# Sixteen 64 x 64 triangular inversions, one factor turned on TensorE instead of multiplied out

## The chip, the cores and the metric

The kernel runs on one core of one Trainium2 chip. The metric is the device time of one execution in microseconds (us), lower is better. It is one long program: two transformer layers, then a third "hybrid" block with a chunked linear recurrence. The change touches one stage of that block.

## The reference, cut to what matters

The hybrid block splits 512 positions into 8 chunks of 64. For every head and chunk a unit lower triangular 64 x 64 system has to be solved before the chunks can be chained:

```python
def _chunk_gated_delta_rule(q, k, v, beta, g):
    ...
    A = jnp.where(strict, jnp.einsum('bhnld,bhnmd->bhnlm', k, k) * decay * beta[..., :, None], 0.0)
    rhs = jnp.concatenate([v * beta[..., None], k * (beta * jnp.exp(gc))[..., None]], axis=-1)
    sol = lax.linalg.triangular_solve(A + jnp.eye(L, dtype=A.dtype), rhs,
                                      left_side=True, lower=True, unit_diagonal=True)
```

The other half of the heads follow the rule of `rwkv7_time_mix`, a step by step scan in the reference, which the kernel brings into the same chunked form with an A of its own.

## The kernel before, in words

The stage is the function `chunk_operators` (names with `ops_` in the trace). It works through 6 **pairs** of heads, i = 0 to 5 (`PAIRS`): pairs 0 to 2 are the RWKV kind, pairs 3 to 5 the gated delta kind (`delta(i)`). A pair has 2 heads h, 8 chunks as 4 tiles t of 2 halves c, so 16 matrices of 64 x 64. A tile of 128 partitions and 512 columns holds all of them: half c of the partitions holds the chunks of parity c, and unit u = 4h + t is a block of 64 columns.

The inverse T of I + A is built in five **levels** (lv 0 to 4), with U, its transpose, kept beside it. Each level takes the part M of A that joins blocks twice as large (POOL, `mask`), and then:

- TensorE (PE), `invert_x`, L2589: XT = M'U, 16 products of 64 x 64;
- ScalarE (ACT), `xt_out`, L2712: XT copied from PSUM to SBUF;
- PE, `invert_p`, L2601: PT = T'XT, and L2606: P = (XT)'T, 16 products each, P not on the last level;
- VectorE (DVE), `update`, L2885: U = U - PT, and L2889: T = T - P.

Between these stand, in an order written out by hand for every engine, the work that finishes the pair before (`finish_wu`, `finish_qm`, `finish_yn` on PE; `wu_out`, `yn_out` on ACT; `qm_out` on DVE) and the work that sets up the next (`setup_*` on PE; `tokens`, `a_out`, `ar_out`, `akr_out`, `init`, `delta_rows` on DVE; `decay_masks`, `diagonal`, `chunk_ends` on POOL). Each engine runs its own list from top to bottom, and semaphores tie the lists together. "Next pair is delta" holds for i = 2, 3, 4: there DVE's `tokens(i + 1)` builds the decays, ACT takes their exponentials, POOL masks them, and POOL's mask for level 3 stands behind those two.

A matrix product written once in the code shows in the trace as two instructions (x32 for 16 products); a transposition shows as one. A product on contraction half c that writes output half c uses two of the array's four quarters over a whole group; the order `DIAG` lets 16 products go round all four quarters, as `finish_qm` (L2542, L2549) does.

Of the kernel before, what the change touches and what calls it, by code (L numbers as in the profile page):

```python
# [20 lines left out]
ALU = mybir.AluOpType  # L21
# [2302 lines left out]
def chunk_operators(k, pi, bi, kr, ki, mt, n0, pc, el, rows, cols):  # L2324
# [5 lines left out]
    with Stage(k, "ops") as st:  # L2330
        slot = [k.H[:, j, :].rearrange("p (u m) -> p u m", m=CHUNK) for j in range(8)]
        A, T, U = slot[0:2], slot[2:4], slot[4:6]
# [12 lines left out]
        XT_B, P_B, PT_B = 0, 1, 2  # L2345
# [3 lines left out]
                 "t_init", "u_init", "chain", "xt_ps", "xt_out", "p_ps", "t_out", "pt_ps", "u_out", "wu_ps", "wu_out", "qm_ps",  # L2349
# [36 lines left out]
        def compact(bk):  # L2386
            return ps[:, bk, :].rearrange("p (u m) -> p u m", m=CHUNK)

# [12 lines left out]
        with k.nc.Block() as block:  # L2401
            @block.tensor
            def _(pe):
# [120 lines left out]
                def finish_wu(i):  # L2524
                    pe.wait_ge(s["u_out"], LV * (i + 1))
                    if not delta(i):
                        pe.wait_ge(s["x1_out"], i + 1)
                    if i:
                        pe.wait_ge(s["yn_out"], 2 * i)
                    for t in range(TT):  # L2530
                        for h in range(2):
                            u = TT * h + t
                            for c in range(2):
                                mm = pe.matmul(units(F0 + h)[half(c), t, :], U[i % 2][half(c), u, :], kx[half(c), i % 2, u, :], start=True, stop=True)
                    mm.then_inc(s["wu_ps"], 1)
# [42 lines left out]
                def invert_x(i, lv):  # L2578
                    n = LV * i + lv
                    pe.wait_ge(s["masked"], n + 1)  # L2580
                    if lv:
                        pe.wait_ge(s["u_out"], n)
                    else:
                        pe.wait_ge(s["u_init"], i + 1)
                        if i:
                            pe.wait_ge(s["xt_out"], n)
                    for u in range(U8):
                        for c in range(2):
                            mm = pe.matmul(compact(XT_B)[half(c), u, :], M[half(c), u, :], U[i % 2][half(c), u, :], start=True, stop=True)  # L2589
                    mm.then_inc(s["xt_ps"], 1)  # L2590

                def invert_p(i, lv):
                    n = LV * i + lv
                    pe.wait_ge(s["xt_out"], n + 1)
                    if lv:
                        pe.wait_ge(s["t_out"], 4 * i + lv)
                    else:
                        pe.wait_ge(s["t_init"], i + 1)
# [13 lines left out]
                for i in range(PAIRS):  # L2612
                    nxt = i + 1 < PAIRS
                    invert_x(i, 0)
                    if i:
                        finish_wu(i - 1)
                    else:
                        setup_akr(0)
# [7 lines left out]
                    invert_x(i, 1)  # L2626
                    if i:
                        finish_yn(i - 1)
# [3 lines left out]
                    invert_x(i, 2)  # L2632
                    if nxt:
                        setup_a(i + 1)
# [3 lines left out]
                    invert_x(i, 3)  # L2638
                    if nxt and not delta(i + 1):
                        setup_akr(i + 1)  # L2640
                    invert_p(i, 3)
                    invert_x(i, 4)
                    if nxt and not delta(i + 1):
                        setup_x1(i + 1)
# [8 lines left out]
            def _(act):  # L2653
# [52 lines left out]
                def xt_out(i, lv):  # L2706
                    n = LV * i + lv
                    act.wait_ge(s["xt_ps"], n + 1)
                    if n:
                        act.wait_ge(s["pt_ps"], n)  # L2710
                        act.wait_ge(s["p_ps"], 4 * i + lv)
                    act.activation(XT, compact(XT_B), ACT.Copy).then_inc(s["xt_out"], 1)  # L2712
# [78 lines left out]
            def _(dve):  # L2791
# [73 lines left out]
                def init(i):  # L2865
                    dve.wait_ge(s["a_out"], 2 * i + 2)
                    if i >= 2:
                        dve.wait_ge(s["wu_ps"], i - 1)
                        dve.wait_ge(s["pt_ps"], LV * (i - 1))
                    dve.tensor_tensor(T[i % 2], A[i % 2], over(level(0)), ALU.mult).then_inc(s["chain"], 1)  # L2870
                    dve.wait_ge(s["ar_out"], 2 * i + 2)
                    if delta(i):
                        dve.tensor_tensor(U[i % 2], ar[:, i % 2, :, 0, :], over(k.c("up0")[:, 0:CHUNK]), ALU.mult).then_inc(s["chain"], 1)
                    chained = i + max(i - MIX_T, 0)
                    dve.wait_ge(s["chain"], chained + 1)
                    dve.tensor_tensor(T[i % 2], over(k.c("ident2")), T[i % 2], ALU.subtract).then_inc(s["t_init"], 1)
                    if delta(i):
                        dve.wait_ge(s["chain"], chained + 2)
                    dve.tensor_tensor(U[i % 2], over(k.c("ident2")), U[i % 2] if delta(i) else ar[:, i % 2, :, 0, :], ALU.subtract).then_inc(s["u_init"], 1)

                def update(i, lv):
                    n = LV * i + lv
                    dve.wait_ge(s["pt_ps"], n + 1)
                    dve.wait_ge(s["u_out"], n) if lv else dve.wait_ge(s["u_init"], i + 1)
                    dve.tensor_tensor(U[i % 2], U[i % 2], compact(PT_B), ALU.subtract).then_inc(s["u_out"], 1)  # L2885
                    if lv < LV - 1:
                        dve.wait_ge(s["p_ps"], 4 * i + lv + 1)
                        dve.wait_ge(s["t_out"], 4 * i + lv) if lv else dve.wait_ge(s["t_init"], i + 1)
                        dve.tensor_tensor(T[i % 2], T[i % 2], compact(P_B), ALU.subtract).then_inc(s["t_out"], 1)  # L2889
# [22 lines left out]
                for i in range(PAIRS):  # L2912
                    nxt = i + 1 < PAIRS
                    if i == 0:
                        akr_out(0)
                    update(i, 0)
                    if i:
# [3 lines left out]
                    update(i, 1)  # L2921
                    if nxt and delta(i + 1):
# [3 lines left out]
                    update(i, 2)  # L2926
                    if nxt:
# [3 lines left out]
                    update(i, 3)  # L2931
                    if nxt:
# [799 lines left out]
```

## Time and profile before

| | |
|---|---|
| median of 3 runs | 2220.4 us (2219.17 to 2224.8) |
| the profiled execution | 2219.96 us, span 2218.2 us |
| the stage, first product to last | 1561.27 to 1733.67 us, 172.4 us |
| PE busy over the span | 97% |
| DVE / ACT / POOL busy over the span | 58% / 41% / 5% |
| mean granted TensorE clock | 0.995 |

The span is the time from the first to the last instruction; a row of the trace gives a start counted from the start of the span.

### The profile page before, as it was taken

Reading aid. Unit: us, or ns where it says so; the run is one execution under the profiler, and the core shown is the slowest. Engines: PE = TensorE matmul, PEld = TensorE weight load, DVE = VectorE, ACT = ScalarE, POOL = GpSimd, SP = SyncE. Lnnn points to the kernel's source line nnn. Section 1 sums busy time; section 2 is a strip of 40 time slices with the busy share of each in tenths; the row PEclk is TensorE's granted clock in tenths of the full one; section 3 lists DMA queues with packets and bytes.
Section 4 is the critical chain, followed back from the end, with each engine's and each line's share of the span. In section 5 each row is a group of like instructions: output and inputs, shape, how many; then the busy total and the mean of one; then the engine's idle time right before and its main releaser. Section 6 shows DMA issues by size and latency. Waiting matters only on the chain. (4 is left out here: it accounts for less than half of the span.)

```text
span 2218.2 us, 35739 instructions
## 1 busy us (share of the span) xinstructions
PE 2156.5 (97%) x14078; PEld 1724.8 (78%) x14078; DVE 1289.6 (58%) x1733; ACT 907.7 (41%) x1421; POOL 119.6 (5%) x96
## 2 busy tenths in 40 slices
PE   8999999999999999999999998999898899999999
PEld 6787788888877777778888876777787566888887
DVE  6564576663377877476665347686465566333333
ACT  4444532222365666642222244654222545323321
POOL 0000011110000000001110000000333000000000
PEclk9999999999999999999999999999999999999999
DMA  6331233333324321323333331322000112333331
GB/s 255 105 117 55 76 114 96 100 97 95 95 77 133 92 65 47 105 76 105 96 100 97 95 95 50 101 85 76 3 4 4 47 39 67 104 95 104 95 95 66
DMA packets 54087, 189.77 MB, mean 86 GB/s; under 512 B 5968, under 2 KB 6224, under 8 KB 53840
## 3 DMA queue, kind: packets, MB, share of 16 engines
q1 hardware_dynamic: 53680, 187.49, 27.5%
q8 instruction: 88, 1.44, 0.3%
q10 hardware_dynamic: 288, 0.59, 0.1%
q14 instruction: 31, 0.25, 0.0%
HBM read 184.91 MB, written 3.15 MB: 85 GB/s over the span
## 5 line engine op out<-in xcount | busy, mean ns | idle before, releaser
L299 PE MATMUL l_banks<-l_r_hi,l_w_hi 128*128 128x512 f32 x1440 | 574.7, 399 | 3.6 <-DVE l_r_lo L1796 2.3
L301 PE MATMUL l_banks<-l_r_hi,l_w_lo 128*128 128x512 f32 x1440 | 561.3, 390 | 0.0
L300 PE MATMUL l_banks<-l_r_lo,l_w_hi 128*128 128x512 f32 x1440 | 561.0, 390 | 0.0
L284 DVE TENSOR_TENSOR l_w_lo<-ring,l_w_hi 128x1024 fp32r<-128x1024 f32 x216 | 299.0, 1386 | 96.8 <-ACT l_w_hi L278 93.0
L278 ACT ACTIVATE l_w_hi<-ring 128x1024 fp32r<-128x1024 f32 x216 | 227.1, 1056 | 291.3 <-PE l_banks L301 286.5
L299 PEld LDWEIGHTS l_banks<-l_r_hi,l_w_hi 128*128 128x128 f32 x1440 | 270.6, 188 | 72.9 <-issue 8.4
L300 PEld LDWEIGHTS l_banks<-l_r_lo,l_w_hi 128*128 128x128 f32 x1440 | 270.8, 188 | 57.9 <-issue 4.3
L301 PEld LDWEIGHTS l_banks<-l_r_hi,l_w_lo 128*128 128x128 f32 x1440 | 270.5, 188 | 57.0
L299 PE MATMUL ff_banks<-ff_r_hi,ff_w_hi 128*128 128x512 f32 x512 | 200.0, 391 | 0.0
L300 PE MATMUL ff_banks<-ff_r_lo,ff_w_hi 128*128 128x512 f32 x512 | 199.2, 389 | 0.0
L301 PE MATMUL ff_banks<-ff_r_hi,ff_w_lo 128*128 128x512 f32 x512 | 199.2, 389 | 0.0
L735 POOL TENSOR_TENSOR tail_mid<-H 128x512 f32 x44 | 60.0, 1363 | 1143.9 <-ACT H L728 772.0
L284 DVE TENSOR_TENSOR ff_w_lo<-ring,ff_w_hi 128x1024 fp32r<-128x1024 f32 x64 | 78.3, 1225 | 61.7 <-ACT ff_w_hi L278 58.4
L299 PEld LDWEIGHTS ff_banks<-ff_r_hi,ff_w_hi 128*128 128x128 f32 x512 | 96.1, 188 | 20.4 <-issue 0.5
L300 PEld LDWEIGHTS ff_banks<-ff_r_lo,ff_w_hi 128*128 128x128 f32 x512 | 96.1, 188 | 20.3 <-issue 0.5
L301 PEld LDWEIGHTS ff_banks<-ff_r_hi,ff_w_lo 128*128 128x128 f32 x512 | 96.1, 188 | 20.2
L292 DVE TENSOR_TENSOR l_r_lo<-tail_mid,l_r_hi 128x512 fp32r<-128x512 f32 x44 | 30.5, 692 | 130.3 <-ACT l_r_hi L288 130.3
L299 PE MATMUL in_acc<-in_r_hi,in_w_hi 128*128 128x512 f32 x216 | 90.9, 421 | 0.0
L288 ACT ACTIVATE l_r_hi<-tail_mid 128x512 fp32r (+1 forms) x44 | 27.7, 630 | 153.1 <-PE l_banks L301 153.1
L301 PE MATMUL in_acc<-in_r_hi,in_w_lo 128*128 128x512 f32 x216 | 85.0, 393 | 0.0
L300 PE MATMUL in_acc<-in_r_lo,in_w_hi 128*128 128x512 f32 x216 | 84.7, 392 | 0.0
L292 DVE TENSOR_TENSOR ff_r_lo<-mid,ff_r_hi 128x512 fp32r<-128x512 f32 x32 | 22.2, 692 | 101.6 <-ACT ff_r_hi L288 101.6
(513 smaller groups left out, 3255.2 us busy)
## 6 DMA issues: line engine op xcount, KB each, us to landing
ring<-weights SPq DMA_DIRECT2D x315, 512.0 KB, 3.6
na_bias<-window_bias SPq DMA_DIRECT2D x16, 512.0 KB, 5.4
da_rel<-t_rel SPq DMA_DIRECT2D x8, 448.0 KB, 4.2
outT<-X SPq DMA_DIRECT2D x12, 256.0 KB, 2.1
X<-xT SPq DMA_DIRECT2D x8, 256.0 KB, 5.7
const<-consts SPq DMA_DIRECT2D x1, 1312.0 KB, 11.5
l_pt<-pT SPq DMA_DIRECT2D x2, 512.0 KB, 4.3
X<-outT SPq DMA_DIRECT2D x4, 256.0 KB, 3.3
```

Of the source, the lines that this page charges most:

```text
L278: act.activation(self.w_hi[:, c % self.slots, :], k.ring[:, g % RING, :], ACT.Copy).then_inc(self.w_rounded, 1)
L284: dve.tensor_tensor(self.w_lo[:, c % self.slots, :], k.ring[:, g % RING, :], self.w_hi[:, c % self.slots, :].bitcast(F32), ALU.subtract).t ...
L288: act.activation(self.hi(slot), src, ACT.Copy).then_inc(self.rhs_rounded, 1)
L292: dve.tensor_tensor(self.lo(slot), src, self.hi(slot).bitcast(F32), ALU.subtract).then_inc(self.rhs_split, 1)
L299: pe.matmul(psum, hi, self.hi(rhs_slot), start=start, stop=False)
L300: pe.matmul(psum, hi, self.lo(rhs_slot), start=False, stop=False)
L301: return pe.matmul(psum, lo, self.hi(rhs_slot), start=False, stop=stop)
L735: pool.tensor_tensor(mid[:, f + j, :], gelu[:, j, :], value[:, j, :], ALU.mult).then_inc(mid_done, 1)
```

## The change

U's columns are ordered tile, head, column, so that the two heads of one tile stand side by side. XT is written to the partition half of its head instead of its chunk, so that `invert_x` and `invert_p` both go over four quarters in the order `DIAG`. T is no longer updated: on every level `turn_u` transposes U, four transpositions of 128 x 128 behind `invert_x`, and DVE copies the result to T (`turned_out`). The product P, the update of T and the making of the first T in `init` are gone. `invert_x` of level 0 now also waits for the last update of the pair before.

```diff
-                    for u in range(U8):
-                        for c in range(2):
-                            mm = pe.matmul(compact(XT_B)[half(c), u, :], M[half(c), u, :], U[i % 2][half(c), u, :], start=True, stop=True)
+                def turn_u(i, lv):
+                    n = LV * i + lv
+                    if lv:
+                        pe.wait_ge(s["u_out"], n)
+                    else:
+                        pe.wait_ge(s["u_init"], i + 1)
+                    if n:
+                        pe.wait_ge(s["t_out"], n)
+                    for t in range(TT):
+                        mm = pe.transpose(units(TURN_B)[:, t, :], U[i % 2][:, :, t, :].rearrange("p h m -> p (h m)"), k.c("ident"))
+                    mm.then_inc(s["t_ps"], 1)
+                def invert_x(i, lv):
+                    n = LV * i + lv
+                    pe.wait_ge(s["masked"], n + 1)
+                    if n:
+                        pe.wait_ge(s["u_out"], n)
+                    if lv == 0:
+                        pe.wait_ge(s["u_init"], i + 1)
+                    for t in range(TT):
+                        for pair in DIAG:
+                            for c, h in pair:
+                                mm = pe.matmul(xt_ps(c, t)[half(h)], M[half(c), TT * h + t, :], U[i % 2][half(c), h, t, :], start=True, stop=True)
                     mm.then_inc(s["xt_ps"], 1)
...
                 def invert_p(i, lv):
                     n = LV * i + lv
                     pe.wait_ge(s["xt_out"], n + 1)
-                    for u in range(U8):
-                        for c in range(2):
-                            mm = pe.matmul(compact(PT_B)[half(c), u, :], T[i % 2][half(c), u, :], XT[half(c), u, :], start=True, stop=True)
+                    pe.wait_ge(s["t_out"], n + 1)
+                    for t in range(TT):
+                        for pair in DIAG:
+                            for c, h in pair:
+                                mm = pe.matmul(pt_ps(h, t)[half(c)], T[i % 2][half(h), 2 * t + c, :], XT[half(h), TT * c + t, :], start=True, stop=True)
                     mm.then_inc(s["pt_ps"], 1)
-                    if lv < LV - 1:
-                        for u in range(U8):
-                            for c in range(2):
-                                mm = pe.matmul(compact(P_B)[half(c), u, :], XT[half(c), u, :], T[i % 2][half(c), u, :], start=True, stop=True)
-                        mm.then_inc(s["p_ps"], 1)
...
+                def turned_out(i, lv):
+                    n = LV * i + lv
+                    dve.wait_ge(s["t_ps"], n + 1)
+                    if n:
+                        dve.wait_ge(s["pt_ps"], n)
+                    dve.tensor_copy(T[i % 2], compact(TURN_B)).then_inc(s["t_out"], 1)
...
                 for i in range(PAIRS):
                     nxt = i + 1 < PAIRS
+                    turned_out(i, 0)
                     if i == 0:
                         akr_out(0)
                     update(i, 0)
+                    turned_out(i, 1)
                     if i:
                         qm_out(i - 1)
                     if nxt and delta(i + 1):
                         delta_rows(i + 1)
                     update(i, 1)
+                    turned_out(i, 2)
                     if nxt and delta(i + 1):
                         tokens(i + 1)
                     if nxt:
                         a_out(i + 1)
                     update(i, 2)
+                    turned_out(i, 3)
                     if nxt:
                         ar_out(i + 1)
                         if not delta(i + 1):
                             akr_out(i + 1)
                     update(i, 3)
+                    turned_out(i, 4)
                     if nxt:
                         init(i + 1)
                     update(i, 4)
```

What stands in a row on an engine moves as follows. On PE, levels 2 and 3 of pair 0, whose next is RWKV; L2414 and in the changed kernel L2430 are `setup_a`, `setup_ar` and `setup_akr`. Before:

```order
L2589 MATMUL ops_ps<-H 64x64 x16
L2414 MATMUL ops_ps<-bi,kr 64x64 x16
L2601 MATMUL ops_ps<-H 64x64 x16
L2606 MATMUL ops_ps<-H 64x64 x16
L2414 MATMUL ops_ps<-kr,bi 64x128 x16
L2589 MATMUL ops_ps<-H 64x64 x16
L2414 MATMUL ops_ps<-kr,ki 64x128 x16
L2601 MATMUL ops_ps<-H 64x64 x16
L2606 MATMUL ops_ps<-H 64x64 x16
```

In the changed kernel, with L2617 for XT, L2604 for the transpositions and L2627 for PT:

```order
L2617 MATMUL ops_ps<-H 64x64 x16
L2604 MATMUL ops_ps<-const,H 128x128 x4
L2430 MATMUL ops_ps<-bi,kr 64x64 x16
L2627 MATMUL ops_ps<-H 64x64 x16
L2430 MATMUL ops_ps<-kr,bi 64x128 x16
L2617 MATMUL ops_ps<-H 64x64 x16
L2604 MATMUL ops_ps<-const,H 128x128 x4
L2430 MATMUL ops_ps<-kr,ki 64x128 x16
L2627 MATMUL ops_ps<-H 64x64 x16
```

The transpositions stand between XT and the set-up product of each level; the second product of `invert_p` is gone.

On DVE, levels 1 and 2 of pair 2, whose next is delta; L2813 to L2825 are `tokens`, L2837 is `a_out`. Before:

```order
L2885 TENSOR_TENSOR H<-H,ops_ps 128x512
L2889 TENSOR_TENSOR H<-H,ops_ps 128x512
L2813 TENSOR_TENSOR ops_akr<-ops_ps,cols 128x512
L2817 TENSOR_SCALAR ops_akr<-ops_akr 128x512
L2819 TENSOR_SCALAR ops_akr<-ops_akr 128x512
L2823 TENSOR_TENSOR ops_kx<-ops_ps,cols 128x8x64 x2
L2825 TENSOR_TENSOR ops_v_tok<-ops_ps,cols 128x2x4x64
L2837 TENSOR_TENSOR H<-ops_ps,ops_akr 128x256 x2
L2885 TENSOR_TENSOR H<-H,ops_ps 128x512
L2889 TENSOR_TENSOR H<-H,ops_ps 128x512
```

In the changed kernel, with L2912 for the update of U, L2906 for the copy of T, L2838 to L2850 for `tokens` and L2862 for `a_out`:

```order
L2912 TENSOR_TENSOR H<-H,ops_ps 128x2x4x64
L2906 COPY H<-ops_ps 128x512
L2838 TENSOR_TENSOR ops_akr<-ops_ps,cols 128x512
L2842 TENSOR_SCALAR ops_akr<-ops_akr 128x512
L2844 TENSOR_SCALAR ops_akr<-ops_akr 128x512
L2848 TENSOR_TENSOR ops_kx<-ops_ps,cols 128x8x64 x2
L2850 TENSOR_TENSOR ops_v_tok<-ops_ps,cols 128x2x4x64
L2862 TENSOR_TENSOR H<-ops_ps,ops_akr 128x256 x2
L2912 TENSOR_TENSOR H<-H,ops_ps 128x2x4x64
L2906 COPY H<-ops_ps 128x512
```

The row ahead of `tokens` was the update of T for level 1 and is now the copy of T for level 2, which needs the transpositions of level 2.

## Rows read from the trace of the kernel before

**Rows 1.** Windows: busy time of each engine over the stage (windows view)

```profile
1561.27:1733.67 172.40, 148.97 (x4524) 134.74 (x4524) 91.94 (x144) 44.17 (x77) 59.39 (x48) 0.98 0.02 4
```

The columns are the stretch, its length, busy time with instructions of PE, PE weight loads, DVE, ACT and POOL, the granted clock, DMA share and GB/s.

**Rows 2.** Timeline of pair 5, level 3: start, duration, engine, line [idle before]

```profile
1719.06 1.15 PE L2589 MATMUL ops_ps<-H 64*64 64x64 f32 x32
...
1720.24 0.60 ACT L2712 ACTIVATE H<-ops_ps 128x512 f32<-128x512 f32 x1 [3.27 <-PE ops_ps L2589]
...
1720.89 1.15 PE L2601 MATMUL ops_ps<-H 64*64 64x64 f32 x32 [0.69 <-ACT H L2712]
...
1722.09 0.69 DVE L2885 TENSOR_TENSOR H<-H,ops_ps 128x512 f32<-128x512 f32 x1 [2.24 <-PE ops_ps L2601]
...
1722.92 1.15 PE L2589 MATMUL ops_ps<-H 64*64 64x64 f32 x32
```

**Rows 3.** Timeline and groups: four-quarter product, copy from PSUM, transpositions

```profile
1729.84 0.69 PE L2542 MATMUL ops_ps<-ops_ar,ops_wu 64*64 64x64 f32 x32 [1.18 <-ACT ops_wu L2693]
...
L1850 DVE COPY tail_m<-l_banks 128x512 f32<-128x512 f32 x8 | 5.3, 685 | 1.4 <-ACT H L1753 1.4
...
1614.49 1.13 PE L2601 MATMUL ops_ps<-H 64*64 64x64 f32 x32
...
1615.55 0.66 PE L2406 MATMUL ops_ps<-const,bi 128*128 128x128 f32 x4
...
1616.57 1.15 PE L2589 MATMUL ops_ps<-H 64*64 64x64 f32 x32
```

**Rows 4.** Timeline of pair 4, level 2 (next pair is delta)

```profile
1689.88 0.69 DVE L2813 TENSOR_TENSOR ops_akr<-ops_ps,cols 128x512 f32<-128x512 f32 x1 [0.57 <-PE ops_ps L2442]
...
1690.79 1.15 PE L2589 MATMUL ops_ps<-H 64*64 64x64 f32 x32
...
1692.76 1.27 POOL L2752 TENSOR_TENSOR ops_akr<-ops_akr,const 128x512 f32<-128x512 f32 x1 [5.62 <-ACT ops_akr L2662]
...
1695.22 1.28 POOL L2770 TENSOR_TENSOR H<-H,const 128x512 f32<-128x512 f32 x1
...
1696.55 0.62 PE L2589 MATMUL ops_ps<-H 64*64 64x64 f32 x14 [0.38 <-POOL H L2770]
```

**Rows 5.** Timeline of pair 1, levels 2 and 3 (next pair is RWKV)

```profile
1603.69 1.09 PE L2589 MATMUL ops_ps<-H 64*64 64x64 f32 x30
...
1608.33 1.10 PE L2589 MATMUL ops_ps<-H 64*64 64x64 f32 x32
1608.57 1.29 DVE L2842 TENSOR_TENSOR ops_ar<-ops_ps,const 128x512 f32<-128x512 f32 x2 [0.22 <-PE ops_ps L2414]
1609.41 1.10 PE L2414 MATMUL ops_ps<-kr,ki 64*64 64x128 f32 x32
...
1610.57 1.29 DVE L2842 TENSOR_TENSOR ops_akr<-ops_ps,const 128x512 f32<-128x512 f32 x2 [0.71 <-PE ops_ps L2414]
...
1612.60 1.15 PE L2589 MATMUL ops_ps<-H 64*64 64x64 f32 x32 [0.24 <-DVE H L2885]
```

**Rows 6.** Timeline of levels 0 and 1: pair 1, and the start of pair 4's level 1

```profile
1590.78 1.15 PE L2589 MATMUL ops_ps<-H 64*64 64x64 f32 x32
1591.76 1.92 PE L2534 MATMUL ops_ps<-ops_kx,H 64*64 64x128 f32 x32
...
1596.31 1.10 PE L2589 MATMUL ops_ps<-H 64*64 64x64 f32 x32
1596.56 0.69 DVE L2902 TENSOR_TENSOR bi<-ops_ps,kr 128x512 f32<-128x512 f32 x1 [0.28 <-PE ops_ps L2549]
...
1684.63 1.09 PE L2589 MATMUL ops_ps<-H 64*64 64x64 f32 x30
```

**Rows 7.** Timeline at the end of pair 3, and a windows row

```profile
1671.12 1.15 PE L2589 MATMUL ops_ps<-H 64*64 64x64 f32 x32
...
1675.48 1.88 PE L2589 MATMUL ops_ps<-H 64*64 64x64 f32 x32 [1.38 <-issue]
...
1675.63:1679.05 3.42, 3.42 (x51) 3.42 (x51) 0.35 (x1) 0.60 (x1) 1.26 (x1) 0.50 0.00 0
```

More of the change, by code:

```diff
@@ L2331, in chunk_operators @@
         slot = [k.H[:, j, :].rearrange("p (u m) -> p u m", m=CHUNK) for j in range(8)]
-        A, T, U = slot[0:2], slot[2:4], slot[4:6]
+        A, T = slot[0:2], slot[2:4]
+        U = [k.H[:, j, :].rearrange("p (t h m) -> p h t m", h=2, m=CHUNK) for j in (4, 5)]
         XT, M = slot[6], slot[7]
@@ L2344, in chunk_operators @@
         ps = st.ps("ps", [P, 8, S])
-        XT_B, P_B, PT_B = 0, 1, 2
+        TURN_B = 2
         SETUP = (3, 4, 7)
@@ L2348, in chunk_operators @@
         names = ("turned", "tok_out", "keys_turned", "key_out", "a_ps", "a_out", "ar_ps", "ar_out", "akr_ps", "akr_out", "x1_ps", "x1_out", "masked",
-                 "t_init", "u_init", "chain", "xt_ps", "xt_out", "p_ps", "t_out", "pt_ps", "u_out", "wu_ps", "wu_out", "qm_ps",
+                 "u_init", "chain", "xt_ps", "xt_out", "t_ps", "t_out", "pt_ps", "u_out", "wu_ps", "wu_out", "qm_ps",
                  "q_out", "mt_out", "yn_ps", "yn_out", "row_ps", "dif_done", "clamped", "exped", "dmask", "scaled", "di_done",
@@ L2387, in compact, with xt_ps, pt_ps, all_xt @@
             return ps[:, bk, :].rearrange("p (u m) -> p u m", m=CHUNK)
+        def xt_ps(c, t):
+            return ps[:, c, t * CHUNK:(t + 1) * CHUNK]
+        def pt_ps(h, t):
+            return ps[:, h, HALF + t * CHUNK:HALF + (t + 1) * CHUNK]
+        def all_xt():
+            return ps[:, 0:2, 0:HALF]
+        def all_pt():
+            return ps[:, 0:2, HALF:S].rearrange("p h (t m) -> p h t m", m=CHUNK)
+        def heads(x):
+            return x.rearrange("p (h t) m -> p h t m", h=2)
         def half(h):
@@ L2533, in finish_wu @@
                             for c in range(2):
-                                mm = pe.matmul(units(F0 + h)[half(c), t, :], U[i % 2][half(c), u, :], kx[half(c), i % 2, u, :], start=True, stop=True)
+                                mm = pe.matmul(units(F0 + h)[half(c), t, :], U[i % 2][half(c), h, t, :], kx[half(c), i % 2, u, :], start=True, stop=True)
                     mm.then_inc(s["wu_ps"], 1)
@@ L2614, in _ @@
                     invert_x(i, 0)
+                    turn_u(i, 0)
                     if i:
@@ L2626, in _ @@
                     invert_x(i, 1)
+                    turn_u(i, 1)
                     if i:
@@ L2632, in _ @@
                     invert_x(i, 2)
+                    turn_u(i, 2)
                     if nxt:
@@ L2638, in _ @@
                     invert_x(i, 3)
+                    turn_u(i, 3)
                     if nxt and not delta(i + 1):
@@ L2642, in _ @@
                     invert_x(i, 4)
+                    turn_u(i, 4)
                     if nxt and not delta(i + 1):
@@ L2710, in xt_out @@
                         act.wait_ge(s["pt_ps"], n)
-                        act.wait_ge(s["p_ps"], 4 * i + lv)
-                    act.activation(XT, compact(XT_B), ACT.Copy).then_inc(s["xt_out"], 1)
+                    act.activation(XT.rearrange("p (c t) m -> p c (t m)", c=2), all_xt(), ACT.Copy).then_inc(s["xt_out"], 1)
                 act.preload_act_table_set(LN_EXP)
@@ L2865, in init @@
                 def init(i):
-                    dve.wait_ge(s["a_out"], 2 * i + 2)
+                    dve.wait_ge(s["ar_out"], 2 * i + 2)
                     if i >= 2:
                         dve.wait_ge(s["wu_ps"], i - 1)
-                        dve.wait_ge(s["pt_ps"], LV * (i - 1))
-                    dve.tensor_tensor(T[i % 2], A[i % 2], over(level(0)), ALU.mult).then_inc(s["chain"], 1)
-                    dve.wait_ge(s["ar_out"], 2 * i + 2)
+                        dve.wait_ge(s["t_ps"], LV * (i - 1))
+                    u0, eye = heads(ar[:, i % 2, :, 0, :]), heads(over(k.c("ident2")))
                     if delta(i):
[L2873 to L2879, printed above, removed]
+                        dve.tensor_tensor(U[i % 2], u0, heads(over(k.c("up0")[:, 0:CHUNK])), ALU.mult).then_inc(s["chain"], 1)
+                        dve.wait_ge(s["chain"], i - MIX_T + 1)
+                    dve.tensor_tensor(U[i % 2], eye, U[i % 2] if delta(i) else u0, ALU.subtract).then_inc(s["u_init"], 1)
+                def turned_out(i, lv):
[4 more added lines that the diff above has]
+                    dve.tensor_copy(T[i % 2], compact(TURN_B)).then_inc(s["t_out"], 1)
                 def update(i, lv):
```

14 lines of the change are left out of this document (1 added, 13 removed).

## The prediction, as put on record before the changed kernel ran

> **What bounds the kernel now.** The page says that PE is busy 97% of the span. That is an average over a program that is nearly all large products. The change lives in one stage, so I read that stage alone: the windows view gives 172.40 us, PE busy 148.97, DVE 91.94, ACT 44.17, POOL 59.39 [rows 1]. PE is busy 86% there, and no engine is full. A stage like that is bound by a chain that passes from engine to engine, so the next view is the timeline, and what I measure in it is the distance from one XT product to the next: the length of a level. There are 30.
>
> The purest level is one with nothing but the inversion in it, in pair 5 [rows 2]. XT starts at 1719.06 and lasts 1.15; ACT starts 0.03 behind its end and takes 0.60; PT starts 0.05 behind that and lasts 1.15; DVE starts 0.05 behind its end and takes 0.69; the next XT starts at 1722.92. Length 3.86. The second product P and the update of T (PE's next in line, and DVE's) lie beside this chain, so their removal by itself gives next to nothing here; it gives something only where PE has set-up work queued behind P.
>
> **The prices of the new pieces.** A group of 16 products over four quarters lasts 0.69 (L2542) [rows 3] against 1.15 over two [rows 2]; it lets the next group start 0.46 earlier as well, so it holds the engine about 0.5 instead of about 1.0. Four transpositions last 0.66. Eight of them, from 1615.55, let the next product start at 1616.57, so four hold PE about 0.58, and the first starts 0.07 later than a plain product would behind the 16 at 1614.49 (0.99 apart) [rows 3]. The copy of a bank from PSUM on DVE takes 0.685 (L1850) [rows 3]. The new DVE and ACT access patterns I take at the old times, 0.69 and 0.60: they move as many elements.
>
> These changes of shape on PE are where a rule speaks against the change. The Trainium skill (TensorEngine Tiling (Array Packing), Key Properties) says that changing the tiling mode drains TensorE, and 30 turns add 60 changes. By the rows above such a pair of changes costs about 0.07 + 0.2, which is inside the 0.65 that I charge; if a change were free, a turn would hold PE about 0.4, and T would be ready 0.1 to 0.2 earlier.
>
> **The new plain level.** Counted from XT's start: XT's last product starts at 0.48, the transpositions start at 0.63 and end at 1.29, DVE copies T from 1.33 to 2.02, PT starts at 2.08 and ends at 2.77, DVE updates U to 3.50, the next XT starts at 3.56. The XT copy on ACT would have let PT start at 0.69 + 0.03 + 0.60 + 0.05 = 1.37, so it is now T, not XT, that comes last, by 0.7. So the shorter products would give 0.9 per level and the turn takes 0.6 back: 3.56 against 3.86.
>
> **The wait that the change adds.** DVE runs its list in order, and the copy of T for level n + 1 stands directly behind the update of U for level n, ahead of all other DVE work of that level. It can't run before the transpositions of that level. So any DVE work of the level starts at XT + 1.95 at the earliest. Before, the row that stood there was the update of T for the level just past, and the other work could start before XT or a quarter of a microsecond behind it. Where that work heads a chain, the level grows. Kind by kind:
>
> 1. *Level 2 with a delta pair next, three levels (i = 2, 3, 4).* Before: `tokens` starts at 1689.88, that is 0.91 before XT at 1690.79. Behind it in a chain: two clamps, two exponentials on ACT (XT's copy waits behind these too), two masks on POOL from 1692.76, then POOL's mask for level 3 at 1695.22 for 1.28, and the next XT at 1696.55, released by it [rows 4]. Length 5.76, all of it set by that chain, 6.67 from `tokens` to XT. After: `tokens` at XT + 1.95, next XT at 1.95 + 6.67 = 8.6. **+2.86 each, +8.6.** This is the largest term.
> 2. *Level 3 with an RWKV pair next, two levels (i = 0, 1).* Before: `ar_out` starts 0.24 behind XT, the `akr` product at 1.08, `akr_out` at 2.24, next XT at 4.27 [rows 5]. After: `ar_out` at 1.95; the `akr` product waits for its first half, 2.65, and lasts 1.15; `akr_out` from 3.85 to 5.14 (two evacuations, 1.29); update of U to 5.76; next XT at 5.8. **+1.55 each, +3.1.**
> 3. *Level 1 with a pair to finish, five levels.* Before, pair 1: `qm_out` starts 0.25 behind XT and `finish_yn` follows at about 1.6 [rows 6]. After: the two evacuations run from 1.95 to 3.24 and `finish_yn` starts at 3.34, 1.7 later. Against that, PT and P, two groups over two quarters, held PE about 1.9 in a row before `setup_tokens`, and now PT alone holds it 0.5 and the change of shape 0.1, 1.3 less: +0.4 for i = 1. For i = 2, 3, 4 the `qm_out` work had been hidden under `setup_rows` and `finish_yn` ran directly behind XT; the length was 6.16 at i = 4 [rows 6, 4]. After, for i = 4: 3.34, plus 1.0 for `finish_yn` (two groups over four quarters), plus 0.6 for PT and the change, plus 2.05 for `setup_tokens` (eight transpositions at 1.02 [rows 3], and four row products that I take as long again) = 7.0, +0.9, and I take the same for i = 2 and 3. For i = 5, without set-up, PT starts at 4.3 and the level ends 1.49 behind it, as in the plain level: 5.8 against the plain chain and 1.0 of `finish_yn`, 4.9: +0.9. **Together +4.0.** Level 1 of pair 0 has nothing to finish and gains 1.1.
> 4. *Level 2 with RWKV next, two levels.* 4.64 before [rows 5], held by PE; `a_out` (two evacuations of half the columns) now fits between the copy of T and the end of PT: 3.56. **-1.1 each, -2.2.**
> 5. *Level 0, five levels (i = 1 to 5).* 5.53 before [rows 6]: XT, then `finish_wu` for 1.92, PT, P, `finish_qm`. After: `finish_wu` from 1.21 to 3.16, its two copies on ACT (0.60 each with a little overlap, 1.1, which P used to hide) to 4.3, `finish_qm` (two groups over four quarters) 1.0: 5.3. **-0.2 to -0.3 each, -1.3.** T's copy is hidden under `finish_wu`.
> 6. *Level 4.* `init` has one operation instead of three (RWKV) or two instead of four (delta). Before 3.97 (1612.60 [rows 5] to 1616.57 [rows 3]) and 4.36 [rows 7]; after 3.78, held by `setup_keys` on PE, and 3.86. **-0.2 for two, -0.5 for three, -0.2 for the last: -2.1.**
> 7. *Plain levels 2 and 3 of pair 5*: -0.3 each, **-0.6.** Level 3 with a delta pair next: `ar_out` (1.29) behind T's copy gives 3.9 against the plain 3.86, **0.**
> 8. *Before the first XT*: two operations fewer in `init` are 1.3, of which POOL's list, which starts its second half at the `akr` product, keeps 0.2: **-1.1.**
>
> Sum: 8.6 + 3.1 + 4.0 - 1.1 - 2.2 - 1.3 - 2.1 - 0.6 - 1.1 = **+7.3 us.** The work removed from PE, some 33 us (in each of six pairs 14 groups of about 1.0 become 10 of 0.5 and 5 turns of 0.65), mostly turns into waiting.
>
> **The clock.** At 1675.63 the granted clock fell to 0.50, the 1.2 GHz level, for 3.42 us [rows 7]; just before, PE had done one product group in 3 us, because of `init`. XT took 1.88 instead of 1.15, and `finish_wu` about 1.0 more: 1.7 us. The level-4 wait shrinks, so this fall may go; but each level of kind 1 now has about 3 us in which PE has nothing between the transpositions and `setup_a`. Three such falls cost between nothing (the POOL chain sets the end there) and 1.7 each; I take 0.8 each and give back 1.7: +0.7. The Trainium skill (TensorE: Matmul & The Clock Gate, Part 1) has an idle or cold engine at half rate, and this trace agrees, by the row above.
>
> The profiled execution took 2219.96 us, 0.4 under the median. 2220.0 + 7.3 + 0.7 = **2228.0 us**, 0.34% over the median. A measurement here can tell about 0.3%, which is 6.7 us, so this is slower by just more than can be told.
>
> **The rivals.**
> - *The gains and losses nearly cancel* (30%). It needs the level-1 terms or the clock to be overstated: if item 3 is 0 instead of +4.0 and no clock falls, 2220.0 + 3.3 - 1.7 = 2221.6. For it: item 3 is the sum of several short overlaps. Against it: item 1 alone is 8.6 and rests on one row order and one chain. Range 2215 to 2226.9.
> - *PE's list is what holds most levels, and 33 us less of it wins* (10%). It would be so if DVE's late start were covered: then items 1 to 3 are no loss, and 2220.0 - 1.1 - 2.2 - 1.3 - 2.1 - 0.6 - 1.1 is 2211.6, and up to 4 less if level 3 gains as level 2 does. For it: PE is 86% busy [rows 1]. Against it: in the pure level of 3.86 PE waits 0.69 for ACT ahead of L2601 [rows 2], and would have to wait for DVE without P. It decides if `tokens` starts less than 0.5 behind XT.
> - *The clock stays low over long stretches* (10%). PE now works 0.5 + 0.6 + 0.5 = 1.6 in a plain level of 3.56 and waits the rest; the fall at 1675.63 came behind such waits. Against it: it came once in 30 levels. At half clock XT, turn and PT are each about 0.4 longer: 1.3 per level. Over 12 levels more that is 2228 + 15 = 2243.
> - *The copy of T collides with POOL's mask*, which starts 0.04 behind XT and lasts 1.27, over the copy (5%). Held until the mask's end, T comes 0.5 later on 29 levels: 2242. Against it: DVE reads PSUM here, and the update of U at 1722.09 took its 0.69 like any other [rows 2].
>
> My forecast itself has 45%, and its own range is 2226 to 2234. With the rivals the range that holds the time 8 times in 10 is 2218 to 2240: the cancelling case is nearly all in, the two slow ones in part, the fast one out. Chances: faster by over 0.3% 0.10, within 0.3% 0.32, slower by over 0.3% 0.58; the forecast lies so near the bound that a part of its own range counts as within.
>
> **What the profile of the changed kernel would show.** PT released by DVE's copy of T and not by ACT, about 2.08 behind XT; plain levels of 3.5 to 3.6; `tokens` (L2838) at about XT + 1.95 and the level-2 lengths of pairs 2, 3, 4 at 8 to 9; L2867's second pair on level 3 of pairs 0 and 1 starting near XT + 3.9; the stage 7 to 8 longer with PE busy some 30 us less. I am wrong if level 2 with delta next is under 6.5 (then the order on DVE isn't what I read), if plain levels are over 4 (collision or clock), or if products over four quarters take much more than 0.69 when PT waits on DVE.

## The result: 31 us slower, and most of it is clock

The changed kernel takes 2251.16 us (median of 4 runs, 2250.37 to 2251.37) against 2219.86: ratio 1.0135, 95% interval 1.0122 to 1.0149. The forecast was 2228 with a range to 2240: right in sign, far too small. Its profiled execution has a span of 2249.6 us.

The windows view of the stage in the changed kernel, with the columns of [rows 1]:

```profile
1561.53:1764.40 202.87, 149.54 (x3876) 124.81 (x3876) 82.81 (x138) 44.46 (x77) 58.34 (x48) 0.77 0.01 3
```

The stage grew from 172.40 to 202.87 us, 30.5 of the 31.4 us by which the span grew. PE has 648 instructions fewer than in [rows 1] and is busy just as long, 149.5 against 149.0 us. The column that moved is the granted clock: 0.98 before, 0.77 now. A busy time that doesn't fall when a seventh of the instructions is taken away is the first sign that each piece takes longer. The trace has the granted clock at 0.50, the 1.2 GHz level, in 92 us of the stage, against 6.8 us before.

A level with nothing but the inversion in it, at that clock, from PE's and DVE's timelines of pair 5 (one piece for each engine):

```profile
1745.12 1.14 PE L2617 MATMUL ops_ps<-H 64*64 64x64 f32 x32 [0.89 <-DVE H L2912]
1746.18 1.11 PE L2604 MATMUL ops_ps<-const,H 128*128 128x128 f32 x4
1748.17 1.13 PE L2627 MATMUL ops_ps<-H 64*64 64x64 f32 x32 [0.88 <-DVE H L2906]
1750.20 1.14 PE L2617 MATMUL ops_ps<-H 64*64 64x64 f32 x32 [0.89 <-DVE H L2912]
...
1747.34 0.69 DVE L2906 COPY H<-ops_ps 128x512 f32<-128x512 f32 x1 [2.36 <-PE ops_ps L2604]
1749.37 0.69 DVE L2912 TENSOR_TENSOR H<-H,ops_ps 128x512 f32<-128x512 f32 x1 [1.34 <-PE ops_ps L2627]
```

```profile
1740.04:1745.12 5.08, 3.31 (x68) 2.66 (x69) 1.38 (x2) 0.60 (x1) 1.27 (x1) 0.50 0.01 3
```

XT, the four transpositions and PT take 1.14, 1.11 and 1.13, where at full clock they take 0.69, 0.66 and 0.69. DVE's two operations still take 0.69. The level is 5.08 long against 3.86 in [rows 2]. XT over four quarters at half clock, 1.14, is no faster than XT over two quarters was at full clock, 1.15. The chain is the one forecast: PT is released by DVE's copy of T (L2906), and XT's copy on ACT no longer matters.

The two largest terms of the queue part of the forecast hold. Pair 3, level 2 (next pair is delta), where [rows 4] had 5.76:

```profile
1671.44 0.69 PE L2617 MATMUL ops_ps<-H 64*64 64x64 f32 x32
1672.06 0.66 PE L2604 MATMUL ops_ps<-const,H 128*128 128x128 f32 x4
1672.76 0.69 DVE L2906 COPY H<-ops_ps 128x512 f32<-128x512 f32 x1 [2.54 <-PE ops_ps L2604]
1673.37 0.68 DVE L2838 TENSOR_TENSOR ops_akr<-ops_ps,cols 128x512 f32<-128x512 f32 x1
...
1675.72 0.77 PE L2430 MATMUL ops_ps<-pi,kr 64*64 64x64 f32 x32 [2.99 <-DVE ops_kx L2848]
...
1676.23 1.27 POOL L2777 TENSOR_TENSOR ops_akr<-ops_akr,const 128x512 f32<-128x512 f32 x1 [12.14 <-ACT ops_akr L2688]
1676.69 1.13 PE L2627 MATMUL ops_ps<-H 64*64 64x64 f32 x32 [0.20 <-ACT H L2737]
...
1678.70 1.26 POOL L2795 TENSOR_TENSOR H<-H,const 128x512 f32<-128x512 f32 x1
1680.02 0.79 PE L2617 MATMUL ops_ps<-H 64*64 64x64 f32 x17
```

`tokens` (L2838) starts 1.93 behind XT (forecast 1.95), the next XT at 8.58 (forecast 8.6). PE stands still for 2.99 us ahead of `setup_a`. The clock falls at 1676.2, inside this level, PT takes 1.13, and the level is not a tenth longer for it, since POOL's masks set its end.

Pair 1, level 3 (next pair is RWKV), where [rows 5] had 4.27:

```profile
1608.60 0.71 PE L2617 MATMUL ops_ps<-H 64*64 64x64 f32 x32
...
1609.93 0.69 DVE L2906 COPY H<-ops_ps 128x512 f32<-128x512 f32 x1 [1.48 <-PE ops_ps L2604]
1610.54 1.28 DVE L2867 TENSOR_TENSOR ops_ar<-ops_ps,const 128x512 f32<-128x512 f32 x2
...
1611.36 1.10 PE L2430 MATMUL ops_ps<-kr,ki 64*64 64x128 f32 x32 [1.47 <-DVE ops_ar L2867]
...
1612.53 1.29 DVE L2867 TENSOR_TENSOR ops_akr<-ops_ps,const 128x512 f32<-128x512 f32 x2 [0.71 <-PE ops_ps L2430]
...
1614.55 0.65 PE L2617 MATMUL ops_ps<-H 64*64 64x64 f32 x29 [1.62 <-DVE H L2912]
```

The `akr` product waits for the first half of `ar_out`, which waits behind the copy of T; 5.95 against a forecast of 5.8.

### The profile page after: what moved, and what is told of

It is laid out like the page before. It is cut to its first block and busy times, and to the rows that moved or that the text cites. A ratio compares the mean times of both kernels' runs of the same rounds, so it can differ in the third digit from the quotient of the medians.

```text
span 2249.6 us, 34468 instructions
## 1 busy us (share of the span) xinstructions
PE 2158.5 (96%) x13430; PEld 1716.0 (76%) x13430; DVE 1280.5 (57%) x1727; ACT 908.3 (40%) x1421; POOL 118.6 (5%) x96
## 5 line engine op out<-in xcount | busy, mean ns | idle before, releaser
L292 DVE TENSOR_TENSOR l_r_lo<-tail_mid,l_r_hi 128x512 fp32r<-128x512 f32 x44 | 30.5, 692 | 130.3 <-ACT l_r_hi L288 130.3
```

The source lines that it names most:

```text
L292: dve.tensor_tensor(self.lo(slot), src, self.hi(slot).bitcast(F32), ALU.subtract).then_inc(self.rhs_split, 1)
```

## The experiments

**Theory:** two causes that add. The copy of T in DVE's list lengthens some levels (15.7 us by items 1 to 3 of the forecast, about 7 once the gains elsewhere are taken off), and PE, which now does its work in short bursts with waits between, is granted the half clock about half of the time (about 24 us). **Rivals:** the new pieces themselves are dear (changes of shape on the array, the copy against POOL's mask); or only one of the two causes is real. Each kernel was timed in five rounds or more beside the kernel before, which ran at 2220.5 to 2221.4.

### Fill the waits of PE

```diff
+                def warm(n, bk, at):
+                    for _ in range(n):
+                        pe.matmul(ps[:, bk, at:at + P], k.c("ident"), k.c("levels")[:, 0:P], start=True, stop=True)
...
                     turn_u(i, 3)
+                    warm(4 if nxt and not delta(i + 1) else 2, F0, 0)
...
                     invert_p(i, 3)
+                    warm(5 if nxt and not delta(i + 1) else 3, TURN_B, 0)
```

and likewise ahead of `finish_yn` (behind a wait for T's copy), on level 2 with a delta pair or none next, and on level 4.

> The changed kernel with products added whose result nobody reads (128 columns each, two to nine in a row), put into waits of PE: after the transpositions and after PT. Nothing else differs, and PE has more work. Clock theory: of the 31 us that the change cost, some 7 are the longer levels and some 24 the granted clock, which was 0.77 over the stage; with the waits filled the clock is at 0.95 or more in the stage and the time 2226 to 2233 us, near the 2228 forecast, although PE does more. Rival, the new pieces themselves are dear (change of shape on the array, copy of T against POOL's mask): the time stays at 2251 or rises by the added work, to 2255 or more.

Measured: 2236.27 us, ratio 1.0069 (1.0056 to 1.0083). Adding work to PE made the changed kernel 15 us faster. The plain level of pair 5 in the filled kernel, where L2632 are the filling products:

```profile
1734.01 0.69 PE L2617 MATMUL ops_ps<-H 64*64 64x64 f32 x32
1734.64 0.66 PE L2604 MATMUL ops_ps<-const,H 128*128 128x128 f32 x4
...
1734.81 1.27 POOL L2810 TENSOR_TENSOR H<-H,const 128x512 f32<-128x512 f32 x1 [2.47 <-PE ops_ps L2617]
...
1735.13 0.61 PE L2632 MATMUL ops_ps<-const 128*128 128x128 f32 x4
1735.33 0.69 DVE L2921 COPY H<-ops_ps 128x512 f32<-128x512 f32 x1 [1.46 <-PE ops_ps L2604]
...
1736.17 0.69 PE L2627 MATMUL ops_ps<-H 64*64 64x64 f32 x32 [0.43 <-DVE H L2921]
...
1736.92 0.69 DVE L2927 TENSOR_TENSOR H<-H,ops_ps 128x512 f32<-128x512 f32 x1 [0.90 <-PE ops_ps L2627]
1737.76 0.69 PE L2617 MATMUL ops_ps<-H 64*64 64x64 f32 x32
```

3.75 in place of 5.08, with the same chain. The four-quarter groups take 0.69, and the copy of T takes its 0.69 beside POOL's mask (L2810), so neither the new pieces nor that meeting is dear. The stage:

```profile
1561.47:1748.38 186.91, 156.77 (x4118) 133.12 (x4118) 82.42 (x138) 44.24 (x77) 58.41 (x48) 0.95 0.01 3
```

The clock is at 0.95 as expected, the time 3 us above the range given: 20 us at half clock are left, three quarters of it on level 1 of pairs 3 and 4, which took 11.55 and 9.68 there. The mean clock over the whole kernel was 0.990 to 0.993 in all five executions, against 0.975 to 0.977 in those of the changed kernel.

A second filling put products where the first had left falls:

```diff
                     invert_p(i, 0)
+                    warm(3 if i else 0, TURN_B, 0)
...
                     turn_u(i, 1)
+                    warm(0 if i else 3, F0, 0)
```

> The changed kernel with filling products put where the first filling left the clock to fall (pair 0 level 1, behind PT on level 0) and one fewer ahead of finish_yn. If the forecast of the schedule (7 us over before) is right and the rest is clock: stage clock over 0.96 and 2226 to 2232 us. If the filled kernel stays at 2236, some 8 us of the change are neither in the forecast's levels nor in the clock.

Measured: 2238.36 us, ratio 1.0076 (1.0062 to 1.0090). A miss: not under 2232. Its stage clock was 0.93, under the 0.96 that its forecast needed, with 27 us at half clock, 16 of them on level 1 of pairs 2 and 4 (10.39 and 10.63; pair 3's was 7.88). So the second filling doesn't settle the last 8 us by its time; the lengths of the single levels do, all but one, below.

### Another order on DVE, alone and with the filling

```diff
                     update(i, 1)
-                    turned_out(i, 2)
                     if nxt and delta(i + 1):
                         tokens(i + 1)
+                    turned_out(i, 2)
                     if nxt:
                         a_out(i + 1)
```

and likewise `qm_out` and `delta_rows` ahead of the copy on level 1, `ar_out` on level 3, `init` on level 4.

> The changed kernel with DVE's list alone in another order: qm_out and delta_rows ahead of the copy of T on level 1, tokens ahead of it on level 2, ar_out on level 3, init on level 4. Queue theory: level 2 with a delta pair next falls from 8.6 to about 5.8, level 3 with RWKV next from 5.9 to about 4.4, level 1 by 1 to 2; the stage is some 20 us shorter as far as the schedule goes. Part of it the clock may take, since PE's list is unchanged and levels of 3.5 leave PE waiting half the time: 2212 to 2232 us. Rival, the order on DVE does not matter and only the clock does: 2245 to 2255 us.

Measured: 2220.69 us, ratio 0.9997 (0.9988 to 1.0006). The four moves give back the whole loss, though the stage's clock is still low:

```profile
1561.29:1736.99 175.70, 140.12 (x3876) 115.76 (x3876) 84.07 (x138) 44.53 (x77) 57.95 (x48) 0.84 0.01 3
```

Level 2 of pair 2 in this kernel, 5.75 long:

```profile
1624.46 0.69 DVE L2838 TENSOR_TENSOR ops_akr<-ops_ps,cols 128x512 f32<-128x512 f32 x1 [0.32 <-PE ops_ps L2458]
...
1625.37 0.69 PE L2617 MATMUL ops_ps<-H 64*64 64x64 f32 x32
...
1627.79 0.68 DVE L2906 COPY H<-ops_ps 128x512 f32<-128x512 f32 x1
...
1631.12 0.58 PE L2617 MATMUL ops_ps<-H 64*64 64x64 f32 x24 [0.75 <-POOL H L2795]
```

`tokens` starts 0.91 ahead of XT again. The gain, 30 us, is more than the 15.7 that items 1 to 3 had put down to the copy's place, for two reasons that this run shows together: the new order also shortens level 1 below what it was before the change (5.78 for 7.78 in pair 2), and 57 us are at half clock instead of 92.

> Both of the edits before together. If the two causes add up: clock 0.95 or more in the stage and 2204 to 2214 us, below the kernel before. If the order alone already keeps PE busy enough, the filling gives nothing or costs up to 5 us against it.

Measured: 2226.42 us, ratio 1.0022 (1.0013 to 1.0031): worse than the new order without filling, outside the range given. The fault is in the edit: on level 1 the filling waits for T's copy, which in this order stands behind `qm_out` and `delta_rows`, so `finish_yn` went behind it too. Level 1 of pair 1 took 7.95 at full clock instead of 5.39, and pairs 2 and 3, with 6.8 us at half clock each, took 10.78 and 10.62 instead of 5.8; level 2 with a delta pair next took 6.45 instead of 5.75. It says nothing on whether the causes add.

> The changed kernel with the copy of T moved from DVE's list to ACT's, behind the copy of XT; DVE's list is as before without the update of T. Queue theory: as with the new order on DVE, level 2 with a delta pair next is at 5.8, level 3 with RWKV next at 4.3 to 4.5, and the time 2212 to 2226 us, with a low clock. If what lengthened those levels was not the copy's place on DVE, they stay at 8.6 and 5.9 and the time at 2245 to 2255.

The edit puts `turned_out` into ACT's list behind `xt_out` and takes it out of DVE's. Measured: 2215.61 us, ratio 0.9979 (0.9968 to 0.9990), inside the range given. Level 2 with a delta pair next is 5.76 and level 3 with RWKV next 4.4 to 4.5: a second way to the same lengths, with DVE's order otherwise untouched. The stage's clock was 0.88 there. What lengthened those levels was the copy's place in DVE's list.

### Keep P, and take P's work away

The four quarters stay, the turn stays on level 0 only, and P and the update of T come back:

```diff
                     mm.then_inc(s["pt_ps"], 1)
+                    if lv < LV - 1:
+                        for t in range(TT):
+                            for c in range(2):
+                                for h in range(2):
+                                    mm = pe.matmul(compact(TURN_B)[half(h), 2 * t + c, :], XT[half(h), TT * c + t, :], T[i % 2][half(h), 2 * t + c, :], start=True, stop=True)
+                        mm.then_inc(s["p_ps"], 1)
...
-                    turn_u(i, 1)
...
                     dve.tensor_tensor(U[i % 2], U[i % 2], all_pt(), ALU.subtract).then_inc(s["u_out"], 1)
+                    if lv < LV - 1:
+                        dve.wait_ge(s["p_ps"], 4 * i + lv + 1)
+                        dve.wait_ge(s["t_out"], n + 1)
+                        dve.tensor_tensor(T[i % 2], T[i % 2], compact(TURN_B), ALU.subtract).then_inc(s["t_out"], 1)
```

> The four-quarter XT and PT are kept, but T is turned from U on level 0 only, and then updated from P as before the change (P over two quarters behind PT, into the bank of the turn; T = T - P on DVE behind the update of U). DVE's list is then nearly that of before. If the turn on every level and its copy were what cost, this is faster than the kernel before: plain levels of 2.9 us in place of 3.86, about 2198 to 2208 us, with the clock at 0.95 or more since P keeps PE at work while DVE updates U. If four-quarter products themselves starve the clock, the stage's clock is 0.8 or so and the time 2215 to 2230 us.

Measured: 2207.20 us, ratio 0.9938 (0.9925 to 0.9952), faster than both kernels. A plain level of pair 5:

```profile
1707.14 0.69 PE L2617 MATMUL ops_ps<-H 64*64 64x64 f32 x32
...
1707.89 0.60 ACT L2740 ACTIVATE H<-ops_ps 128x512 f32<-128x512 f32 x1 [2.80 <-PE ops_ps L2617]
...
1708.54 0.69 PE L2627 MATMUL ops_ps<-H 64*64 64x64 f32 x32 [0.71 <-ACT H L2740]
1709.06 1.10 PE L2633 MATMUL ops_ps<-H 64*64 64x64 f32 x32
...
1709.30 0.69 DVE L2915 TENSOR_TENSOR H<-H,ops_ps 128x512 f32<-128x512 f32 x1 [1.47 <-PE ops_ps L2627]
1710.14 0.65 PE L2617 MATMUL ops_ps<-H 64*64 64x64 f32 x29
```

3.00 us. PT is released by ACT again at XT + 1.40; P (L2633) lies under DVE's update of U and costs the chain nothing. The stage is 158.4 us long at clock 0.97. So the four-quarter products are worth 0.86 on a plain level, and the turn on every level took 0.74 of it back (3.74 at full clock).

> The kernel that keeps P (2207 us), with work left out: on levels 1 to 3 only 2 of the 16 products of P are made, so T is updated from stale values and the output isn't the reference's. P lies beside the chain (DVE updates U meanwhile), so by the schedule this gives 0 to 2 us: 2205 to 2207 if the clock stays. Clock theory: P is what kept PE at work in those 18 levels, so the granted clock falls more often and the time RISES though work is taken away: 2210 to 2225 us, stage clock under 0.93. This is the reverse of the filling.

Measured: 2208.92 us, ratio 0.9947 (0.9933 to 0.9960), against 2207.20 and 0.9938 (0.9925 to 0.9952) with the work in. It lies under the range that the clock theory gave, and the two intervals overlap.

```profile
1562.16:1723.50 161.34, 126.22 (x4044) 108.28 (x4044) 84.82 (x138) 44.23 (x77) 58.04 (x48) 0.87 0.01 3
```

The clock part came as expected: 0.87, with 43 us at half clock instead of 10, and over the whole kernel 0.986 to 0.988 in all five executions against 0.993 to 0.995. The rise in time did not come: 1.7 us is too little to tell. Some levels were shorter at full clock (3.16 for 3.98 on level 1 of pair 0), and that paid for most of the clock. What it shows: with 504 PE instructions taken away the clock falls, and no time is gained.

> The kernel before with the same left out: on levels 1 to 3 only 2 of the 16 products of P, so the output isn't the reference's. It shows what P's removal alone is worth to the old kernel. Schedule: 5 to 7 us less, where PE had set-up work queued behind P: 2213 to 2215 us if the clock stays. Clock theory: some more falls than the one of before, each about 1.5 us where PE is on the path, since XT and PT over two quarters still hold PE 2 of 3.9 us: 2214 to 2222 us.

Measured: 2214.12 us, ratio 0.9970 (0.9961 to 0.9979), stage clock 0.98 as before, 6.8 us at half clock as before: the schedule's share came and no more time at half clock. So taking P away was not enough to bring the clock down where XT and PT went over two quarters; in the kernel with four quarters it was.

> The changed kernel with the order of its products alone altered: XT and PT do all the products of one diagonal first and then those of the other, so that only two quarters are in use at a time. Same products, same turn, same queues; a group holds PE about 1.0 us instead of 0.5. By the schedule at full clock that is 0.9 us more in each of about 25 levels, over 2250 + 20. Clock theory: a group over four quarters at half clock took 1.13 us in the changed kernel, no less than one over two quarters at full clock before (1.15), so the longer groups cost little where the clock was low and keep it high: stage clock over 0.93, time 2245 to 2262 us. Rival (the low clock comes from something else than how much of the time PE works): clock stays near 0.77 and the time goes over 2270.

```diff
-                    for t in range(TT):
-                        for pair in DIAG:
+                    for pair in DIAG:
+                        for t in range(TT):
```

Measured: 2260.57 us (2250.96 to 2264.60), ratio 1.0176 (1.0160 to 1.0193). In the profiled execution, 2251 us like the changed kernel's, XT over two quarters took 0.97 at full clock, and the plain level 4.30 against 3.74, so the nominal price is 0.28 a group, 60 groups, 17 us and not the 0.9 a level that I had expected; 9 of them were paid in the median and none in the profiled execution. Two groups of pair 5, level 3, and the stage:

```profile
1746.06 0.97 PE L2617 MATMUL ops_ps<-H 64*64 64x64 f32 x32 [0.88 <-DVE H L2912]
...
1748.49 0.98 PE L2627 MATMUL ops_ps<-H 64*64 64x64 f32 x32 [0.88 <-DVE H L2906]
```

```profile
1561.76:1763.68 201.92, 151.98 (x3876) 129.87 (x3876) 82.88 (x138) 44.20 (x77) 58.37 (x48) 0.89 0.01 3
```

The clock rose from 0.77 to 0.89, short of the 0.93 expected, with 46 us at half clock for 92. But this is the fastest of the five executions. Over the whole kernel its mean clock is 0.985, the other four had 0.977 to 0.984, the slower the lower, and the changed kernel had 0.975 to 0.977. So the clock rose clearly in two of the five and little in the others (median 0.979). How long PE is at work between the waits is thus at most part of the cause; with waits of the same 0.88 us as in the changed kernel, pair 5 ran at full clock up to its last XT in this execution.

### POOL's order

```diff
-                    if nxt and delta(i + 1):
-                        decay_masks(i + 1)
                     mask(i, 3)
+                    if nxt and delta(i + 1):
+                        decay_masks(i + 1)
```

> The kernel that keeps P, with POOL's mask for level 3 ahead of the two decay masks of the next pair. In the trace of the kernel that keeps P, level 2 with a delta pair next is still 5.76, as before the change, set by POOL. Expected: these three levels at about 4.9, 2 to 3 us in all, 2203 to 2206 us. If ACT's exponentials ahead of the XT copy set them as well, nothing: 2207.

Measured: 2203.92 us, ratio 0.9926 (0.9913 to 0.9940): the fastest median, 17 us under the kernel before, though its interval overlaps that of the kernel that keeps P. Level 2 with a delta pair next went from 5.76 to 5.11, 5.11 and 4.90, 2.2 us in all; two stretches of 3.4 us at half clock, on pair 1 and on pair 5, were gone too, which is chance or consequence, I can't tell which.

> The kernel before with only POOL's mask for level 3 ahead of the next pair's two decay masks. It says how much of the gain of that edit has nothing to do with the change. Expected: level 2 with a delta pair next from 5.76 to 5.3 or less, 1 to 2.5 us in all, 2218 to 2220 us.

Measured: 2221.57 us, ratio 1.0005 (0.9995 to 1.0014): nothing, and above the range given. The three levels did go to 5.32 and 5.33, and 13 us of the stage were at half clock instead of 6.8, six of them on level 0 of pair 0, which took 7.39 for 5.46.

## Why the prediction was wrong, step by step

The lengths of the levels, at full clock where any of the changed kernel and its two filled forms had them so (XT to XT, us):

| kind of level | before | forecast | changed, full clock |
|---|---|---|---|
| plain (pair 5, levels 2 and 3) | 3.86 | 3.56 | 3.74 |
| level 2, delta next, three | 5.76 | 8.6 | 8.6 |
| level 3, RWKV next, two | 4.28 | 5.8 | 5.9 |
| level 2, RWKV next, two | 4.63 | 3.56 | 3.74 |
| level 1, pair 0 | 4.88 | 3.8 | 3.81 |
| level 1, pair 1 | 7.38 | +0.4 | 7.93 |
| level 1, pairs 2 and 3 | 7.78, 8.06 | +0.9 | 7.95, 7.88 |
| level 1, pair 4 | 6.16 | 7.0 | none at full clock; 9.68 at best |
| level 1, pair 5 | 4.90 | 5.8 | 5.86 |
| level 0, pairs 1 and 5 | 5.53, 5.50 | 5.3 | 5.34 |
| level 0, pairs 2 to 4 | 7.53, 7.53, 9.15 (3.4 of it at half clock) | 5.3 | 7.36, 7.43, 7.36 |
| level 4, RWKV / delta next | 3.97 / 4.37 | 3.78 / 3.86 | 3.80 / 4.04 |

- **The queue terms (items 1 to 8) held as a sum.** Over the 29 distances between the 30 XTs the kernel before adds up to 155.4 us, or 153.7 with its one level at half clock taken at the 7.53 of its like. The changed kernel adds up to 183.9, and the lowest lengths of the three runs to 165.8, 2.7 of which are what the one level never seen at full clock took over its forecast of 7.0. With the first XT 1.6 us earlier in the stage, the schedule alone costs 8 to 10.5 us. The forecast was 7.3. The largest item, 1, came to the tenth (2.8 to 2.9 each). That the sum is so near is in part luck: item 3 was some 1.6 too dear if pair 4 took its 7.0, and items 4 to 7 promised some 2 us more than came.
- **The latency from DVE to PE** was taken as 0.06. Where PT and XT wait for DVE alone, it is 0.15 (U's update ends at 1737.61, XT starts at 1737.76 in the filled kernel). The plain level was 0.18 short for that. [rows 2] had 0.14 there (1722.09 + 0.69 to 1722.92), though with P in PE's list.
- **Item 3 was a little too dear**: +0.9 for pairs 2 and 3 was -0.2 to +0.2.
- **Item 5 misread three levels.** It took 5.53 for all five; level 0 of pairs 2 to 4, with set-up of a next pair in it, was 7.5. The gain was about the same, 0.1 to 0.2.
- **The failed step is "The clock".** It read the one fall of [rows 7] as the price of long waits only, gave the changed kernel three falls, in the levels of kind 1, and +0.7 us. There were 92 us at half clock. The stage grew by 30.5, of which 8 to 10.5 are the schedule, so the clock cost 20 to 23 us more than before. Of the three levels that it named, two lost nothing by the clock, as its lower bound had it, because POOL sets their end, and pair 4's lost 0.6 (9.23 for 8.63). The time went elsewhere, by each level's length less its lowest at full clock, pair 4's level 1 taken at 7.0: some 11 us on levels 0 and 1, where PE also finishes one pair or sets up the next, 6 on level 4 and on level 3 ahead of a next pair, 1.3 on each plain level, and 3.6 behind the last XT (14.2 us to the end of the stage, 10.6 in the filled kernel).
- **The third rival, "the clock stays low over long stretches", is what happened.** Its price for a plain level was right, 1.3 (5.08 against 3.74). Its chance, 10%, and its count, 12 levels, were not: 20 of the 29 levels had time at half clock. The argument against it, that the fall had come once in 30 levels, came from a kernel in which PE had P to do while DVE worked and whose groups held PE twice as long. The change takes away both, and the runs point to both: without most of P the kernel before kept its clock at 0.98, the one with four quarters fell from 0.97 to 0.87. Filling PE's waits gave 15 us back and so shows the cause; the new order on DVE and the copy on ACT show the second cause. The one run made to show that the two add had a fault of its own, so that they add is not shown.
- **The fourth rival, the copy of T against POOL's mask, is out**: the copy took 0.69 with the mask beside it (1735.33 and 1734.81 in the filled kernel).
- **The rule of the Trainium skill on changes of tiling mode** (TensorEngine Tiling (Array Packing), Key Properties) was weighed in the forecast and has no part in the miss: at full clock the turn held PE and delivered T as the rows of before said, T's transpositions ending 1.29 behind XT in the filled kernel.
- What stays open: level 1 of pair 4. The filled kernel was 8 us over the forecast; 5.7 us of its profiled execution lie in four levels that had time at half clock and were shorter by that much at full clock in another run, and 2.7 in this one, which no run had at full clock. Nor does any run put products in place of the transpositions, so whether a transposition keeps the clock up as a product does is not shown.

## What to carry to other kernels

When a change makes PE's pieces shorter in a stage where PE already waits, work out what PE does between its waits before and after, not only the length of the chain: work that lies beside the chain, like P here, may be part of what keeps the clock up, and to turn it into waiting can cost more than the shorter products give. It did so together with shorter pieces, and not alone. Look at where a new copy stands in an in-order list before adding it: one copy of 0.69 us put at the head of a level's work on DVE lengthened three levels by 2.8 us each, and moving it behind gave it all back. Take the parts of a change one by one: four quarters with the turn on level 0 only were 14 us faster than before, and with it on every level 31 us slower.

## What the runs showed of the hardware that I had not expected

- PE at half clock in nearly half of a stage, in a kernel on a single core: 92 of 203 us. A group of 16 products over four quarters then takes 1.13 to 1.14 us, four transpositions 1.11, 16 products of 64 x 128 (L2550) 3.37 against 1.92 in [rows 6].
- Products without a reader raised the clock of the stage from 0.77 to 0.95 and took 15 us off the kernel.
- The Trainium skill (TensorE: Matmul & The Clock Gate, Part 1) has an idle array at half rate. Here it stayed low where PE was never idle for long: in pair 5 of the changed kernel the clock fell at 1737.6, behind waits of 0.72 and 2.07 us, and stayed at 0.50 to 1758.1, over three levels in which PE waited 0.9 us at a time, for each copy of T and each update of U.
- The executions of one kernel can differ by their clock: the one over two quarters took 2251.0 at a mean clock of 0.985 and 2264.6 at 0.977, the one with the copy on ACT 2210.6 at 0.994 and 2224.8 at 0.983. The kernel before lies within 6 us, and the changed one, with the lowest clock of all, within 1 us.
